# Down projection of a SwiGLU block: plain tiling replaced by seven products of operand sums

## What is computed

```python
D_FF = 2816
def reference(...):
    ...
    x = x + rms_norm(mix, g_post_mix[l])
    h = rms_norm(x, g_pre_ffn[l])
    f = (jax.nn.silu(h @ w_gate[l]) * (h @ w_up[l])) @ w_down[l]
    x = x + rms_norm(f, g_post_ffn[l])
    return x
```

## Time and profile before

| | us |
|---|---|
| median of three runs | 2527.95 |
| lowest and highest run | 2527.36, 2533.58 |
| profiled execution, device time | 2531.92 |
| profiled execution, span on the core | 2530.1 |

### The profile page before, as it was taken

The page is one execution under the profiler, slowest core; times in us unless marked ns, Lnnn a source line. Parts: engine busy times, 40 slices in busy tenths (PEclk is TensorE's granted clock), DMA queues, the critical chain, the costliest instruction groups (busy, mean ns, idle before and its releaser), DMA issues.

```text
span 2530.1 us, 35402 instructions
## 1 busy us (share of the span) xinstructions
PE 2461.7 (97%) x12312; PEld 2076.7 (82%) x12312; DVE 1257.7 (50%) x2460; ACT 871.4 (34%) x1751; POOL 625.5 (25%) x397
## 2 busy tenths in 40 slices
PE   7999999999999799998999999899999999999998
PEld 6888888889999688886788888688888878888886
DVE  4331456625556577778656656766666531101101
ACT  4301122227777322325444444544444321000000
POOL 0099555533345567760000000000000000000000
PEclk9999999999999899999999999999999999999999
DMA  5413123367775445563433233342332355424333
GB/s 184 147 47 117 58 90 117 124 189 180 181 175 154 145 152 177 170 207 123 133 125 108 95 128 125 98 168 95 123 113 95 103 201 175 158 99 159 119 140 108
DMA packets 259255, 342.03 MB, mean 135 GB/s; under 512 B 18256, under 2 KB 162256, under 8 KB 258896
## 3 DMA queue, kind: packets, MB, share of 16 engines
q1 hardware_dynamic: 259152, 340.67, 43.3%
HBM read 222.76 MB, written 117.83 MB: 135 GB/s over the span
## 4 chain that ended last, share of the span: by engine, by line
PE 49%; DVE 2%; DMA 1%; issue 1%; ACT 1%; POOL 0%; SPq 0%; POOLq 0%; DVEq 0%; ACTq 0%
PE fin_psum_bank L1749 31%; PE fin_psum_bank L1825 18%; DVE ff_b_lo L2038 1%; DMA ff_raw<-in_w_gate 1%; DVE ff_total L2228 0%; DVE ff_w_lo L2034 0%; DVE ff_total L2232 0%; POOL ff_ssq L2030 0%; DMA out<-ff_total 0%; ACT ff_b_hi L1864 0%; DMA ff_acts<-a_lo 0%; DVE ff_up L2107 0%; ACT ff_taken L1892 0%; ACT ff_squares L2020 0%; DVE ff_raw L2048 0%
## 5 line engine op out<-in xcount | busy, mean ns | idle before, releaser
L1749 PE MATMUL fin_psum_bank<-ff_b_hi,ff_w_hi 128*128 128x512 f32 x1232 | 483.6, 393 | 19.5 <-ACT ff_taken L1892 7.3
L1749 PE MATMUL fin_psum_bank<-ff_b_lo,ff_w_hi 128*128 128x512 f32 x1232 | 482.5, 392 | 0.0
L1749 PE MATMUL fin_psum_bank<-ff_b_hi,ff_w_lo 128*128 128x512 f32 x1232 | 482.1, 391 | 0.0
L1825 PE MATMUL fin_psum_bank<-ff_down_hi,ff_acts 128*128 128x512 f32 x1408 | 436.1, 390 | 8.1 <-DVE ff_down_lo L2215 4.5
L2030 POOL TENSOR_TENSOR ff_ssq<-ff_ssq,ff_minus_half 128x1 f32<-128x1 f32 x16 | 8.8, 548 | 1341.3 <-DVE ff_ssq L2219 1341.3
L1825 PEld LDWEIGHTS fin_psum_bank<-ff_down_hi,ff_acts 128*128 128x128 f32 x1408 | 265.1, 188 | 65.4 <-issue 4.9
L1749 PEld LDWEIGHTS fin_psum_bank<-ff_b_hi,ff_w_hi 128*128 128x128 f32 x1232 | 233.1, 189 | 71.3 <-ACT ff_taken L1892 9.0
L1825 PE MATMUL fin_psum_bank<-ff_down_lo,ff_acts 128*128 128x512 f32 x704 | 274.6, 390 | 0.0
L1749 PEld LDWEIGHTS fin_psum_bank<-ff_b_hi,ff_w_lo 128*128 128x128 f32 x1232 | 233.1, 189 | 49.0
L1749 PEld LDWEIGHTS fin_psum_bank<-ff_b_lo,ff_w_hi 128*128 128x128 f32 x1232 | 233.2, 189 | 48.4
L460 PE MATMUL pr_psum_acc<-pr_hT_hi,pr_w_hi 128*128 128x512 f32 x512 | 199.2, 389 | 0.0
(11 more groups left out here) (182 smaller groups left out, 4297.5 us busy)
## 6 DMA issues: line engine op xcount, KB each, us to landing
ff_raw<-in_w_gate SPq DMA_DIRECT2D x22, 1024.0 KB, 6.4
ff_raw<-in_w_up SPq DMA_DIRECT2D x22, 1024.0 KB, 5.7
a_hi<-ff_a_hi SPq DMA_DIRECT2D x88, 256.0 KB, 2.1
a_lo<-ff_a_lo SPq DMA_DIRECT2D x88, 256.0 KB, 2.4
ff_acts<-a_hi SPq DMA_DIRECT2D x88, 256.0 KB, 2.8
ff_acts<-a_lo SPq DMA_DIRECT2D x88, 256.0 KB, 3.2
att_out<-at_orow SPq DMA_DIRECT2D x192, 66.0 KB, 3.1
mx_att_in<-att_out SPq DMA_DIRECT2D x16, 792.0 KB, 4.8
```

The costliest lines, as they stand in the source:

```text
L1749: last = nc.tensor.matmul(to, w[:, i, k, :], b[i][:, k, :], start=fresh and k == 0 and which == 0, stop=k == KH - 1 and which == 2, skip_g ...
L1825: last = nc.tensor.matmul(bank[:, ORDER[b], :], acts[n % 4][:, part, c * P:(c + 1) * P], w[k][:, half * GROUP:(half + 1) * GROUP], start=k ...
```

## The change

The down projection gets the form of the gate and up stage. Its activations A are cut by feature tiles (even k, odd k, in 11 pairs) and by token group within a half; `w_down` by even and odd tile and by column half. Seven products, in the order P1, P5, P6, P4, P7, P3, P2, each over eight tiles of 128 tokens (`TOKENS`), each tile one bank that gets 11 pairs by three matmuls, 33 in a row: 7 x 8 x 11 x 3 = 1848 matmuls of the same shape. `TILES` is 56.

- In the gate and up stage the splitting of `up` goes (`high_a`, `low_a`). DVE makes four sums and differences of the four blocks instead (`add_acts`, into `a_sum`), and SP stores seven operands, unsplit, 256 KB each: P1, P4 and P2 straight from `up`, the other four from `a_sum`. They lie in DRAM as `a_parts`, so that a strip's store goes in runs of 128 floats (512 B), and a tile's load is contiguous by partition (5.6 KB).
- In the down stage each tile's operand (128 by 1408, 704 KB) is loaded (`load_act`), rounded (`high_act`) and split (`low_act`) two tiles ahead, in a ring of three. Each product's weights come once more from DRAM, 22 loads of 256 KB where the operand is a difference of two blocks (P5, P7), 11 where it is one block or a block less the running difference, and are summed (`sum_down`, P5, P6, P4, P7) and split (`high_down`, `low_down`) during the product before, into the other of two sets.
- The results are gathered in SBUF, in `near` and `far`, eight tiles each of 128 by 1024. The first two products are copied out of PSUM by ACT (`copy_out`), the others added by DVE (`lift`; two instructions each for P4 and P7).
- Rows are finished in SBUF instead of PSUM: the eight far row blocks during P7 and P3 (steps 34 to 44), the near ones during P2, one a tile, the last behind the last tile. `squares`, scaling, x1 and store are as before in size.
- The weights of the first product are loaded and split before the gate and up stage ends, in part within its last turns.

```diff
     def sync(sp):
+        def load_act(t):
+            o, n = divmod(t, TOKENS)
+            i = PRODUCTS[o]
+            if t >= 3:
+                sp.wait_ge(tile_done, t - 2)
+            sp.wait_ge(stored[i], 16 * PARTS * (n // 4 + 1))
+            sp.dma_start(act_raw[t % 3][:], D["a_parts"][i, n]).then_inc(act_loaded[t % 3], 16)
...
             if half:
+                sp.wait_ge(w_lo_done[P4], ALL - 1)
+                sp.wait_ge(w_lo_done[P3], ALL - 1)
+                load_down(0, 3)
+                load_down(0, 4)
                 sp.wait_ge(w_lo_done[P4], ALL)
                 sp.wait_ge(w_lo_done[P3], ALL)
+                load_down(0, 5)
+                load_down(0, 6)
+                load_act(1)
+                sp.wait_ge(done[P1], ALL)
+                for k in range(7, PAIRS):
+                    load_down(0, k)
+            store(at + PARTS - 1, half, P4)
+            store(at + PARTS - 1, half, P2)
+            store_sums(at + PARTS - 1, half)
+        sp.wait_ge(done[P3], ALL)
+        for t in range(TILES):
+            o, n = divmod(t, TOKENS)
+            if t + AHEAD < TILES:
+                load_act(t + AHEAD)
+            if o + 1 < len(PRODUCTS):
+                if o and n == 0:
+                    sp.wait_ge(tile_done, TOKENS * o)
+                for k in PAIRS_OF[n]:
+                    load_down(o + 1, k)
...
+            if t + 1 in FINALS:
+                load_x1(FINALS[t + 1])
+            if t - 1 in FINALS:
+                store_out(FINALS[t - 1])
...
+        for t in range(TILES):
+            o, n = divmod(t, TOKENS)
...
+            if 0 < o <= COPIED:
+                pe.wait_ge(copied, TOKENS * (o - 1) + n + 1)
+            elif o:
+                pe.wait_ge(lifted, TOKENS * (o - 1 - COPIED) + n + 1)
+            pe.wait_ge(act_lo_done, t + 1)
+            for k in range(PAIRS):
+                if n == 0:
+                    pe.wait_ge(down_lo_done, PAIRS * o + k + 1)
+                for which, (a, w) in enumerate(((act_hi, down_hi), (act_hi, down_lo), (act_lo, down_hi))):
+                    last = nc.tensor.matmul(bank[:, ORDER[n], :], a[t % 3][:, k, :], w[o % 2][k][:],
+                                            start=k == 0 and which == 0, stop=k == PAIRS - 1 and which == 2)
+            last.then_inc(tile_done, 1)
...
     def vector(dve):
-        def low_a(n, c):
-            dve.wait_ge(a_hi_done, 2 * n + TURN[c])
-            nc.vector.tensor_tensor(a_lo[:, c, :], up[:, c, :], a_hi[:, c, :].bitcast(F32), ALU.subtract).then_inc(a_lo_done, 1)
+        def add_acts(n):
...
+            nc.vector.tensor_tensor(to[0], at[C12], at[C22], ALU.add).then_inc(a_sum_done, 1)
+            nc.vector.tensor_tensor(to[1], at[C11], at[C12], ALU.subtract).then_inc(a_sum_done, 1)
...
+            nc.vector.tensor_tensor(to[2], to[0], at[C11], ALU.subtract).then_inc(a_sum_done, 1)
...
+            nc.vector.tensor_tensor(to[3], at[C21], to[2], ALU.subtract).then_inc(a_sum_done, 1)
...
             else:
                 direct(n)
-                low_a(n - 1, C22)
+                for k in range(3, 7):
+                    low_down(dve, 0, k)
                 merge(n, 1, C12)
-                low_a(n - 1, C21)
-                low_a(n - 1, C12)
+                for k in range(7, PAIRS):
+                    low_down(dve, 0, k)
+                low_act(dve, 1)
+                add_acts(n - 1)
...
+        for t in range(TILES + 1):
+            o, n = divmod(t, TOKENS)
+            if t > COPIED * TOKENS:
+                lift(t - 1)
+            if o + 1 < len(PRODUCTS):
+                for k in PAIRS_OF[n]:
+                    sum_down(dve, o + 1, k)
+            if t + AHEAD < TILES:
+                low_act(dve, t + AHEAD)
+            if o + 1 < len(PRODUCTS):
+                for k in PAIRS_OF[n]:
+                    low_down(dve, o + 1, k)
+            if t in FINALS:
+                finish(FINALS[t])
```

390 lines of the change are left out of this document (223 added, 167 removed).

## The result

The changed kernel took 2470.97 us, the median of 4 runs (2469.90 to 2472.31); the kernel before took 2529.41 beside it. The ratio is 0.9765, 95% interval 0.9753 to 0.9776: 58.4 us faster. The profiled execution of the change took 2469.9 us with a span of 2468.0. Before it was 2531.9 with a span of 2530.1, so the profiled executions lie 62.0 us apart.

A forecast was written before the change was run, and what follows sets the result against it. PE bounds the kernel, the down stage by its number of matmuls. Terms -59.8 - 4.4 - 4.7 + 3.9 + 1.0 - 0.8 + 1.3 = -63.5 us: 2468.4 against the profiled 2531.9, 2464.5 against the median; range 2457 to 2482.

The forecast's parts named there:

- The count: Down stage on PE: 2112 - 1848 = 264 fewer matmuls at 0.2267 us each, all on the path, -59.8 us.
- Tile 2: Early down stage: operand loaded behind the last strip's sum stores, low part behind two weight differences; PE waits +3.9 us.
- The slow start: PE at the lower clock after a gap: the old 1.7 us stay, behind tile 2's wait, so 0 in the sum.
- Tile 1: Start of down: DVE finishes tile 1's low part at 2038.3, PE wants it at 2040.0; no wait, 1.7 us to spare.
- Later tiles: Rest of down: load, rounding and split take 11 us of 14.96 available; +1.0 us allowed for DVE running late.
- DMA shares: Gate and up rises from 0.35 to 0.40, P7 0.64 at 220 GB/s; transfers covered, at no cost.
- The middle: Where gate and up's halves meet: raw weights load earlier behind less DVE work and fewer stores, -0.8 us (-2 to +1.5).
- Tile 2 in time: Rival, chance 0.10: weights are there early, stall and slow start vanish, 3.9 + 1.7 us less, 2459.
- Transfers that bind: Rival, chance 0.07 including costs in between: down's 83 MB at 178 GB/s take 466 us instead of 419, so 2512.
- The ring: Rival, chance 0.03: loop of load, ACT and DVE over two tiles sets down's pace; at 18 us, kernel 2550.
- A slow start after every short gap: Rival, chance 0.02: three gaps of about a microsecond at product changes each lose 1.7 us at 1.2 GHz, 2469.5.
- A matmul that costs more in a long run: Down, 33 matmuls in a row on one bank: 1848 x 0.01 us is 18 us; chance counted with transfers that bind.

The follow-up runs named there:

- plus5: Changed kernel with five more matmuls of the same shape per tile (38 for 33), 2128 in all: 2531.6 us, ratio 1.0006 to the kernel before.
- control: The changed kernel run again without edits, beside three edited versions on the same chip: 2472.3 us, ratio 0.9773 to the kernel before.
- order: Changed kernel with the operand's low part ahead of the weights' differences on DVE: 2470.5 us, ratio 0.9764 to the kernel before.
- first: Changed kernel with tile 2's operand load issued ahead of the last strip's sum stores on SP: 2470.8 us, ratio 0.9760 to the kernel before.
- both: Changed kernel with low part ahead of weight differences (DVE), loads for tiles 2 and 3 ahead of the sums' stores (SP): 2464.1 us, ratio 0.9742.
- pairs5: Changed kernel with six of eleven feature pairs left out of every tile's matmuls, all loads, splits and sums kept: 2345.1 us, down 295.0 us.

## Why the prediction was right, and where it was off

All in us, profile to profile:

| term | predicted | measured |
|---|---|---|
| 264 matmuls | -59.8 | -59.8 |
| gap at the boundary | -4.4 | -4.6 |
| old waits in down | -4.7 | -4.7 |
| wait at tile 2 | +3.9 | +6.3 |
| slow start after it, and the ends of the short waits | 0 | +0.9 |
| wait at tile 1 | 0 | +1.1 |
| later tiles | +1.0 | 0 |
| gate and up, with the middle | -0.8 | -2.7 |
| stages ahead | 0 | +0.9 |
| tail | +1.3 | +0.6 |
| sum | -63.5 | -62.0 |

- *The count.* Right, by plus5 and by the steady windows. A run of 33 matmuls on one bank costs per matmul what a run of 12 did.
- *Tile 2.* The mechanism was right, named with its place and engines, and 2.4 us too small. Counted from the stage's first matmul (2030.5, where I had 2032.5), the operand's load went out 12.9 us in, where I had 8.9. Of these 4.0 us, 2.9 are the last sum, which came late because DVE had stood for the weights of pairs 7 to 10 (the failed step below). The other 1.1 are SP, which took 1.47 us to issue that sum's store, for which I had nothing. The load landed in 4.8 us for my 5.5, and the low part was ready 3.8 us later than I had it. PE came 1.4 us later too, most of it by its wait at tile 1, and so the wait is 2.4 us longer. The bounds of 1.4 and 9 us hold it. Of the control's 6.4 us, *order* still waits 4.9 and *first* 5.5, and *both* nothing: SP's order and DVE's each suffice for most of the wait. The prediction named both, but priced the chain through DVE alone.
- *The slow start.* I took it as long as before, 1.7 us, which is what the starts of before give. By starts it was 2.2 us here and 3.0 in the control, and *both* saves 2.9 us beside the waits. The other 0.4 of the row's 0.9 are what two waits cost beyond their brackets. The same explains the 1.1 us of the old stage that I had not placed: four short waits, each some 0.3 us longer than its bracket.
- *Tile 1.* This step failed: "No wait, with 1.7 us to spare." I had counted DVE's passes from data in SBUF, 7.8 us from the end of the last direct product to the end of tile 1's low part; it took 10.5 (2028.70 to 2039.22). The loads of pairs 7 to 10 go out only when the low part of pair 3 is made, and ACT and DVE wait for the landing. The condition stands in the code (`load_down` waits for `down_lo_done`, and pair k lands on the semaphore of pair k - 4), and I passed over it. It cost 1.1 us at tile 1 and most of the miss at tile 2. This is read from the trace; no run issues these loads earlier, and *both* still waits 0.98 us there.
- *Later tiles.* Nothing at all, and *pairs5* says why: everything but PE needs 5.3 us of a tile's 7.48 on average, and 6.5 in the tightest product.
- *DMA shares.* For the runs of 512 B I had the share of gate and up rise from 0.35 to 0.40. It stayed at 0.35: a packet of 512 B takes 27 ns in the trace, where I had estimated 36. P7 moved 233 GB/s (2279.9 to 2339.8) where I had 220, and the highest 50 us of the down stage before were 225 GB/s (2037 to 2087), not 211. Nothing in the sum hung on these.
- *The middle.* In the right direction, and larger. Of gate and up's 2.7 us, 0.5 lie in its first 50 us, where the eleven executions with the changed gate and up scatter by 1.1 us. The middle has 2.1, and 2.1 to 3.0 in the eleven: 1.3 us or more beyond my 0.8, and just outside my bounds of -2 to +1.5. Before there were two long gaps on PE there:

```profile
1608.92 0.76 PE L1749 MATMUL fin_psum_bank<-ff_b_hi,ff_w_hi 128*128 128x512 f32 x1 [4.73 <-issue]
...
1640.65 0.50 PE L1749 MATMUL fin_psum_bank<-ff_b_hi,ff_w_hi 128*128 128x512 f32 x1 [3.02 <-ACT ff_taken L1892]
```

  besides the 1.33 us of the earlier trace rows. Now there is one:

```profile
1618.54 0.77 PE L1799 MATMUL fin_psum_bank<-ff_b_hi,ff_w_hi 128*128 128x512 f32 x1 [8.59 <-issue]
```

  That is 0.5 us less of gap (8.59 for 9.08) and one slow start fewer. The order on ACT shows why. Two rows of before, then one of now; L1892 and L1940 copy a bank that PE waits for, L1886 rounds an operand for the down stage:

```profile
1607.70 0.63 ACT L1886 ACTIVATE ff_a_hi<-ff_up 128x512 fp32r<-128x512 f32 x1 [3.69 <-DVE ff_up L2111]
1608.24 0.58 ACT L1892 ACTIVATE ff_taken<-fin_psum_bank 128x512 f32<-128x512 f32 x1
...
1602.71 0.58 ACT L1940 ACTIVATE ff_taken<-fin_psum_bank 128x512 f32<-128x512 f32 x1
```

  The rounding, for which ACT stood 3.69 us, is gone; PE gets its bank 5.5 us sooner and runs on to the next point, which it leaves when it did before (1618.54 for 1618.30). The slow start that follows now makes it reach the product ahead of 1640 at 1637.64 instead of 1634.74, so it no longer has to wait 3.02 us there (where the slow start is only 1.5 us long, as in the control, 0.3 to 0.5 us of wait are left). The old wait had brought the lower clock again, a loss of 1.7 us by its starts (a window of before):

```profile
1641.00:1645.00 4.00, 4.00 (x12) 3.14 (x11) 1.29 (x2) 0.63 (x2) 0.00 (x0) 0.57 0.69 207
```

  My reason for a gain was another, an earlier load of the raw weights, and it was not it: they were issued at 1624.07 (1623.92 before), 0.2 us earlier at most when counted from the last gap ahead of the middle (1593.33 for 1593.00). This account is read from the two traces; no run isolates it.
- *The rivals.* Tile 2 in time: not in the change, but *both* makes it come about, and its 2464.1 in the change's place is 8.2 us lower, where I had priced 5.6. Transfers that bind: refuted, by 210 and 229 GB/s over 60 us without a wait, and by 303 in pairs5. The ring: refuted, the floor is 5.3 us a tile on average and not over 8.6. A slow start after every short gap: refuted, the 1.1 us at tile 1 kept the clock at 1.00 (the next two starts follow after 0.33 and 0.23 us). A matmul that costs more in a long run: refuted by the windows.
- *The total.* 2464.5 against 2471.0. Of the 6.5 us, 1.5 are the sum. The other 5 are the baseline: I took off 4.0 because the profiled execution of before lay that far above the median shown, while that of the change lay 1.1 below its own. With more runs the kernel before has a median of 2528.6 to 2530.2 in the later sessions, so 1.5 us of the 4.0 was the median of three runs being low. That the sum itself is off by no more than 1.5 us is in part luck: the terms missed by 5.3 us in one direction and by 3.8 in the other.
